# Dealing out anew the work of the opening stage of a hybrid attention layer in fp32

## The chip, the cores and the metric

One core of a Trainium2 chip runs the whole layer. The metric is the device time in microseconds (us). The engines are TensorE (PE, with its weight loads PEld), VectorE (DVE), ScalarE (ACT), GpSimd (POOL) and SyncE (SP), which here issues nearly all DMAs.

## What is computed

```
h = rms_norm(x, g_pre);  proj = h @ w_in        # 512 tokens, D = 2048
mkv = rms_norm(mem, g_mem) @ w_mem_kv           # 256 memory tokens, 4 heads of K and V
A: 6 heads, block-sparse causal attention with a T5 bias
B: 6 heads, log_f = log_sigmoid(fb + b_forget), c = cumsum(log_f),
   causal softmax(q k^T * scale + c_i - c_j) v
C: 4 heads, attention into the 256 memory tokens
y = concat(A * silu(ga), B * silu(gb), C * silu(gm));  out = x + rms_norm(y @ w_out, g_post)
```

## The kernel before, in words

**Precision and products.** Every fp32 operand is split in a high part (fp32r) and the rest. A matmul of full precision is three (lines 674 to 676: high by high, low by high, high by low). ScalarE makes the high part of a weight piece of 128 x 1024 (L1018), VectorE subtracts it for the low part (L1429), both into one of three ring slots; each slot's high part waits for the product three earlier (`used`).

**Large loop.** Projections are made by a seven-product scheme over halves of rows and columns (TOK_A to TOK_G), for 28 pairs of columns; pairs 0 to 3 are the memory heads' q and gate. A product is 8 x 3 matmuls. VectorE also adds the weight sums (L1456) and ScalarE and VectorE move partial results (c_ps is seeded from d_ps, L1116). During pair p the attention of the pair before runs between products. For memory heads: scores after product A, row maxima on VectorE after A, exp on ScalarE at B, reciprocal and normalisation at C, transposes after E, high and low parts of pT at E, probability times V (L821) after G, the gate product `gated` (L1556) on VectorE.

**Opening.** PE turns the memory tokens (8 banks, L741); ScalarE scales and writes their high part (`hi_memory`, L1075), VectorE the low part (`lo_memory`, L1516). Then eight strips (STRIPS_MEM) give K and V of the memory tokens: `strip(t)` waits for `mem_free`, which says that the PSUM bank of two strips before was read (k_mem, L1665, for strips 0 to 3; vT, L1601, `copy_v_mem`, for 4 to 7). Beside strips 3 to 6 the x tokens are turned by quarters (`turn_tiles`, `TURN_DURING`; from the twelfth bank on a turn waits for `bank_taken` of four banks before) and both engines take them from PSUM (`take_tokens`, L1089 to L1097 on ScalarE, L1533 on VectorE). Squares of a token tile (L1060) and its scaling (L1508) lie in strips 0 to 4. In strip t ScalarE makes the high part of the first piece of strip t+1, copies k_mem to kmv (L1226, after `mem_free`), then makes the second high part; VectorE does k_mem, scaling, the low part of kmv, then both low parts. The memory norms are spread over columns by one PE matmul after strip 1's first half (L853), from rstd_diag (L1695).

**Late tokens.** TOK_B, C, E, G are sums of quarters, split in high and low parts of 128 x 2048 by `hi_late` (L1106) and `lo_late` after the strips, in the order of LATE_ORDER; G - C is made at L1713. Between them stand the turned V of the memory heads (`hi_v_mem`, `lo_v_mem`).

**Forget gates.** wf holds the weights, cleared by a memset (L1700), in four parts; PE multiplies A, D, F and E tokens by them (L883) before pair 0. ScalarE copies 6 rows (L1258), VectorE forms z (L1722), POOL works out -|z| (L1939, L1940), ScalarE takes exp (L1272), POOL adds 2 (L1943), VectorE takes the reciprocal (L1744, end of pair 1), POOL runs a series of 20 operations of 6x512 (L1945 to L1953), and VectorE scans (L1747, end of pair 3).

The order on each engine is written out by hand; an engine works strictly in that order, so what stands behind a wait waits too.

Of the kernel before, what the change touches and what calls it, by code (L numbers as in the profile page):

```python
# [15 lines left out]
P = 128  # L16
# [55 lines left out]
LATE_ORDER = [TOK_E, TOK_B, TOK_C, TOK_G]  # L72
# [104 lines left out]
def build(nc, x, mem, w_in, b_forget, w_mem_kv, w_out, g_pre, g_post, g_mem, rel_bias, buckets, out):  # L177
    ctx = ExitStack()
    with ctx:
# [59 lines left out]
        wf, _ = place("wf", [P, 4, KH, 38], F32R, at=vT_at + 4 * NMEM)  # L239
# [108 lines left out]
        f_rec = sem("f_rec")  # L348
# [322 lines left out]
        def _(pe):  # L671
# [9 lines left out]
            def strip(t, between):  # L681
# [3 lines left out]
                for half in range(2):  # L685
                    pe.wait_ge(lo_done, 2 * t + half + 1)
                    w = weights(2 * t + half)
                    for k in range(KH):
                        kt = KH * half + k
                        last = three(d_ps[t % 2][:, 0:NMEM], (w[:, 0, k], w[:, 1, k]), (memT[:, 0, kt], memT[:, 1, kt]),  # L690
                                     kt == 0, kt == KT - 1)
# [184 lines left out]
            pe.wait_ge(bank_taken, TURNS)  # L876
# [139 lines left out]
        def _(act):  # L1016
# [62 lines left out]
            def take_tokens(pair, half):  # L1079

                for b in range(4 * half, 4 * half + 4):
                    act.wait_ge(bank_turned, 8 * pair + b + 1)
                    for j in range(2):
# [12 lines left out]
                        else:  # L1096
                            last = act.activation(tok[:, WHOLE[TOK_F], 0, k], src, ACTF.Copy, scale=g)  # L1097
                    last.then_inc(bank_hi, 1)

            def hi_late(i):  # L1100
                if i == LATE_ORDER[0]:
                    act.wait_ge(used, MEM_PIECES)
                    act.wait_ge(bank_taken, TURNS)
                if i == TOK_G:
                    act.wait_ge(late_f32, 1)
# [110 lines left out]
            for t in range(STRIPS_MEM):  # L1216
# [10 lines left out]
                hi_next(1)  # L1227
                if t == 0:
# [189 lines left out]
        def _(dve):  # L1418
# [91 lines left out]
            def lo_memory(half):  # L1510

                for b in range(4 * half, 4 * half + 4):
# [9 lines left out]
            def take_tokens(pair, half):  # L1522

                for b in range(4 * half, 4 * half + 4):
                    dve.wait_ge(bank_hi, 8 * pair + b + 1)
                    for j in range(2):
# [8 lines left out]
                        if (pair, half) != (2, 0):  # L1535
                            i, by = {(1, 0): (TOK_A, g_neg), (1, 1): (TOK_D, g), (2, 1): (TOK_F, g)}[(pair, half)]
# [118 lines left out]
            dve.tensor_scalar(gains_neg[:], gains[:, 1], -1.0, None, ALU.mult).then_inc(gain_negated, 1)  # L1655
            for t in range(STRIPS_MEM):
                if t == 1:
# [347 lines left out]
```

## Time and profile before

| | us |
|---|---|
| median of 3 runs | 935.55 |
| lowest, highest | 934.09, 936.16 |
| the profiled execution's own time | 932.82 |
| its span, first to last instruction | 931.0 |

The mean granted clock of TensorE was 0.987 of full speed. The profile covers one execution; its stretch from 0 to about 94 us is the opening, from there to 215.7 lie the memory pairs 0 to 4. Instructions are given as start, duration, engine, line, operation, out<-in and, in brackets, how long the engine was idle before and what ended that. An instruction's duration includes some 0.1 us in which the next has already begun on VectorE and ScalarE; costs of a list of work are taken from start to start.

### The profile page before, as it was taken

What the parts mean: (1) busy time and instruction counts of PE and PEld (TensorE: products, weight loads), DVE (VectorE), ACT (ScalarE), POOL (GpSimd) and SP (SyncE); (2) the same over time, 40 slices, a digit from 0 to 9 for tenths busy, and PEclk for the clock granted to TensorE, in tenths of its full rate; (3) what the DMA queues carried; (4) which work ended last, traced back from release to release, by engine and by line L of the source; (5) the groups of instructions that cost most, each with busy time, mean ns of one, the idle gap of its engine ahead of it and who ended that gap; (6) DMA issues with size and microseconds to landing.
All of it is one profiled execution on the core that took longest, in us unless ns stands there. A gap on an engine that the chain in (4) does not pass through costs nothing.

```text
span 931.0 us, 16276 instructions
## 1 busy us (share of the span) xinstructions
PE 887.5 (95%) x6525; PEld 839.5 (90%) x6525; DVE 728.4 (78%) x997; ACT 503.4 (54%) x882; POOL 76.7 (8%) x71
## 2 busy tenths in 40 slices
PE   7997998999999999999999999999999998889994
PEld 5887998999999999999999999999999886667873
DVE  5889878888777777777777777777777758998967
ACT  5785555555545454555555555555464645644452
POOL 0000408600000000000010202010111000000000
PEclk9998999999999999999999999999999998999998
DMA  9951424343333433343434343525252897276664
GB/s 301 294 136 46 147 58 103 102 115 102 103 102 104 102 103 102 103 103 102 110 96 114 91 122 83 134 72 144 73 146 59 281 300 239 58 269 238 227 237 168
DMA packets 166673, 130.08 MB, mean 140 GB/s; under 512 B 6393, under 2 KB 143257, under 8 KB 165446
## 3 DMA queue, kind: packets, MB, share of 16 engines
q1 hardware_dynamic: 166310, 127.99, 47.6%
q8 instruction: 52, 0.85, 0.4%
q10 hardware_dynamic: 288, 1.05, 0.4%
q14 instruction: 23, 0.19, 0.1%
HBM read 120.87 MB, written 9.73 MB: 140 GB/s over the span
## 4 chain that ended last, share of the span: by engine, by line
PE 73%; DVE 16%; ACT 5%; issue 4%; DMA 2%; DVEq 0%; POOL 0%; ACTq 0%; POOLq 0%
PE d_ps L674 11%; PE d_ps L676 11%; PE d_ps L675 11%; PE e_ps L674 6%; PE e_ps L676 6%; PE e_ps L675 6%; DVE ring L1429 5%; PE c_ps L674 3%; PE c_ps L676 3%; PE c_ps L675 3%; PE pt_ps L821 3%; DMA raw<-in_w_out_dram 2%; DVE sums L1456 1%; ACT ring L1018 1%; PE score_ps L675 1%
## 5 line engine op out<-in xcount | busy, mean ns | idle before, releaser
L1429 DVE TENSOR_TENSOR ring<-sums,ring 128x1024 fp32r<-128x1024 f32 x121 | 151.1, 1249 | 98.4 <-ACT ring L1018 97.8
L1429 DVE TENSOR_TENSOR ring<-raw,ring 128x1024 fp32r<-128x1024 f32 x131 | 161.3, 1235 | 59.5 <-ACT ring L1018 59.0
L674 PE MATMUL d_ps<-tok_hi,ring 128*128 128x256 f32 x672 | 191.8, 285 | 2.9 <-DVE ring L1429 2.9
L676 PE MATMUL d_ps<-tok_lo,ring 128*128 128x256 f32 x672 | 190.8, 284 | 0.0
L675 PE MATMUL d_ps<-tok_hi,ring 128*128 128x256 f32 x672 | 190.7, 284 | 0.0
L1018 ACT ACTIVATE ring<-raw 128x1024 fp32r<-128x1024 f32 x131 | 137.9, 1058 | 76.7 <-PE d_ps L676 36.2
L1018 ACT ACTIVATE ring<-sums 128x1024 fp32r<-128x1024 f32 x121 | 127.4, 1053 | 26.1 <-DVE sums L1456 17.7
L674 PEld LDWEIGHTS d_ps<-tok_hi,ring 128*128 128x128 f32 x672 | 129.4, 193 | 3.3 <-issue 3.3
L675 PEld LDWEIGHTS d_ps<-tok_hi,ring 128*128 128x128 f32 x672 | 129.5, 193 | 0.0
L676 PEld LDWEIGHTS d_ps<-tok_lo,ring 128*128 128x128 f32 x672 | 129.5, 193 | 0.0
L1456 DVE TENSOR_TENSOR sums<-raw 128x1024 f32<-128x1024 f32 x56 | 69.9, 1248 | 0.1
L1456 DVE TENSOR_TENSOR sums<-sums,raw 128x1024 f32<-128x1024 f32 x56 | 69.9, 1248 | 0.0
L674 PE MATMUL c_ps<-tok,ring 128*128 128x256 f32 x224 | 64.4, 288 | 0.0
L674 PE MATMUL e_ps<-tok_hi,ring 128*128 128x256 f32 x224 | 64.3, 287 | 0.0
L674 PE MATMUL e_ps<-tok,ring 128*128 128x256 f32 x224 | 64.3, 287 | 0.0
L676 PE MATMUL e_ps<-tok_lo,ring 128*128 128x256 f32 x224 | 63.4, 283 | 0.0
L675 PE MATMUL d_ps<-tok,ring 128*128 128x256 f32 x224 | 63.4, 283 | 0.0
L676 PE MATMUL d_ps<-tok,ring 128*128 128x256 f32 x224 | 63.4, 283 | 0.0
L676 PE MATMUL c_ps<-tok,ring 128*128 128x256 f32 x224 | 63.4, 283 | 0.0
L674 PE MATMUL d_ps<-tok,ring 128*128 128x256 f32 x224 | 63.4, 283 | 0.0
L675 PE MATMUL e_ps<-tok_hi,ring 128*128 128x256 f32 x224 | 63.4, 283 | 0.0
L675 PE MATMUL c_ps<-tok,ring 128*128 128x256 f32 x224 | 63.4, 283 | 0.0
(337 smaller groups left out, 2198.9 us busy)
## 6 DMA issues: line engine op xcount, KB each, us to landing
raw<-in_w_in_dram SPq DMA_DIRECT2D x112, 512.0 KB, 5.5
raw<-in_w_out_dram SPq DMA_DIRECT2D x48, 512.0 KB, 5.2
raw<-in_w_mem_kv_dram SPq DMA_DIRECT2D x16, 512.0 KB, 8.4
stage<-in_x_dram SPq DMA_DIRECT2D x4, 1024.0 KB, 9.5
xres<-in_x_dram SPq DMA_DIRECT2D x4, 1024.0 KB, 7.4
out_dram<-o_sb SPq DMA_DIRECT2D x16, 256.0 KB, 2.6
y_dram<-ybuf SPq DMA_DIRECT2D x15, 256.0 KB, 2.3
sums<-in_w_out_dram SPq DMA_DIRECT2D x6, 512.0 KB, 6.8
```

The source lines that it names most:

```text
L674: pe.matmul(dst, lhs[0], rhs[0], start=start, stop=False, skip_group_check=True)
L675: pe.matmul(dst, lhs[1], rhs[0], start=False, stop=False, skip_group_check=True)
L676: return pe.matmul(dst, lhs[0], rhs[1], start=False, stop=stop, skip_group_check=True)
L821: last = pe.matmul(bank[:, first:S], v, pT[:, hl_p, kb, first:S] if not head.memory else pT_mem[:, hl_p, kb, first:S], start=(hl_v, hl_p, ...
L1018: act.activation(dst, src, ACTF.Copy).then_inc(hi_done, 1)
L1429: return dve.tensor_tensor(dst, a_, hi_.bitcast(F32), ALU.subtract)
L1456: dve.tensor_tensor(sum_tile(p, s), one, two, ALU.add).then_inc(sum_done, 1)
```

## The change

- PE waits for the memory tokens by bank in strip 0, not for four and for eight banks; VectorE makes the first weight pieces' low parts between the banks.
- In strips 1 to 7 VectorE makes the low part of the first piece of the next strip ahead of everything else (`lo_next(t, 0)`).
- The two table copies go from VectorE to ScalarE (strip 5). wf moves to other space and POOL clears it, after 16 turned banks.
- Of the last token quarter (2, 1) ScalarE writes F's high part and C from PSUM; VectorE then does E - C and F's low part as two whole operations; C + B follows after the strips. LATE_ORDER is B, C, E, G.
- The forget gates' E part goes behind pair 0's product D; the copy and z behind product E, the exp behind product G.
- The series goes from POOL to VectorE, one operation (12 in all; scalar and tensor steps fused) after each product of pair 2 and the first five of pair 3.

```diff
-LATE_ORDER = [TOK_E, TOK_B, TOK_C, TOK_G]
+LATE_ORDER = [TOK_B, TOK_C, TOK_E, TOK_G]
...
-        wf, _ = place("wf", [P, 4, KH, 38], F32R, at=vT_at + 4 * NMEM)
+        wf, _ = place("wf", [P, 4, KH, 38], F32R, at=pT_at)
...  PE
                         kt = KH * half + k
+                        if t == 0 and k % 2 == 0:
+                            pe.wait_ge(bank_taken, kt // 2 + 1)
...
-                if t == 0:
-                    pe.wait_ge(bank_taken, 8)
...
-            pe.wait_ge(bank_taken, 4)
...
-            pe.wait_ge(bank_taken, TURNS)
+            pe.wait_ge(bank_hi, TURNS)
             pe.wait_ge(wf_ready, 1)
...
             turn_v_mem(NM - 1)
+            pe.wait_ge(bank_taken, TURNS)
             forget_gates(3, TOK_F, slice(T2, S))
             pe.wait_ge(v_ready, NM - 1)
             pe.matmul(c_ps[:, 0:T2], tok[:, 0, 0, 0, 0:P], tok[:, 0, 0, 0], start=True, stop=True)
-            pe.wait_ge(late_ready, 1)
-            forget_gates(2, TOK_E, slice(T2, S), final=True).then_inc(f_done, 1)
...
                     product(p, i)
+                    if p == 0 and i == TOK_D:
+                        pe.wait_ge(late_ready, LATE_ORDER.index(TOK_E) + 1)
+                        forget_gates(2, TOK_E, slice(T2, S), final=True).then_inc(f_done, 1)
                     attention(p, i)
...  ACT
                         else:
-                            last = act.activation(tok[:, WHOLE[TOK_F], 0, k], src, ACTF.Copy, scale=g)
+                            act.activation(tok[:, WHOLE[TOK_F], 0, k], src, ACTF.Copy, scale=g)
+                            last = act.activation(token_f32(TOK_C)[:, k], src, ACTF.Copy, scale=g)
...
                 hi_next(1)
+                if t == NM + 1:
+                    for i, (bank, lo_, hi_) in enumerate(table_banks):
+                        act.wait_ge(table_made, i + 1)
+                        act.activation(table[:, lo_:hi_], bank[0:NA, 0:hi_ - lo_], ACTF.Copy).then_inc(table_copied, 1)
...
-            hi_late(TOK_E)
             hi_v_mem(2)
+            hi_late(TOK_B)
             hi_operand(0, 2)
-            hi_late(TOK_B)
             hi_v_mem(3)
             hi_late(TOK_C)
+            hi_late(TOK_E)
             hi_late(TOK_G)
-            act.wait_ge(f_done, 1)
-            act.activation(fbuf[:, 1], f_ps[32:32 + NB, :], ACTF.Copy).then_inc(f_low, 1)
...
-                if p == 0 and i == TOK_D:
+                if p == 0 and i == TOK_E:
+                    act.wait_ge(f_done, 1)
+                    act.activation(fbuf[:, 1], f_ps[32:32 + NB, :], ACTF.Copy).then_inc(f_low, 1)
+                if p == 0 and i == TOK_G:
                     act.wait_ge(f_neg, 1)
                     act.activation(fbuf[:, 1], fbuf[:, 2], ACTF.Exp).then_inc(f_exp, 1)
...  DVE
+                if (pair, half) == (2, 1):
+                    dve.wait_ge(bank_hi, TURNS)
+                    dve.tensor_tensor(token_f32(TOK_E), token_f32(TOK_E), token_f32(TOK_C), ALU.subtract
+                                      ).then_inc(late_f32, 1)
+                    minus(tok[:, WHOLE[TOK_F], 1], token_f32(TOK_C), tok[:, WHOLE[TOK_F], 0]).then_inc(bank_taken, 4)
+                    return
...
-                        if (pair, half) == (2, 1):
-                            scaled(token_f32(TOK_C)[:, k], g, token_f32(TOK_B)[:, k], ALU.add)
-                            last = scaled(token_f32(TOK_E)[:, k], g_neg, token_f32(TOK_E)[:, k], ALU.add)
...
-            lo_memory(0)
+            lo_memory(0, 2)
             lo_mem(0)
+            lo_memory(2, 4)
             lo_mem(1)
-            lo_memory(1)
+            lo_memory(4, 8)
...
+            def lo_next(t, half):
+                if t + 1 < STRIPS_MEM:
+                    lo_mem(2 * (t + 1) + half)
+                else:
+                    add_weights(0, half + 1)
+                    lo_operand(0, half)
+
             for t in range(STRIPS_MEM):
+                if t > 0:
+                    lo_next(t, 0)
...
-                for half in range(2):
-                    if t + 1 < STRIPS_MEM:
-                        lo_mem(2 * (t + 1) + half)
-                    else:
-                        add_weights(0, half + 1)
-                        lo_operand(0, half)
-                if t == NM + 1:
-                    for i, (bank, lo_, hi_) in enumerate(table_banks):
-                        dve.wait_ge(table_made, i + 1)
-                        dve.tensor_copy(table[:, lo_:hi_], bank[0:NA, 0:hi_ - lo_]).then_inc(table_copied, 1)
+                if t == 0:
+                    lo_next(t, 0)
+                lo_next(t, 1)
...
-                    dve.memset(wf[:].bitcast(F32), 0.0).then_inc(wf_cleared, 1)
...
+            lo_v_mem(2)
             dve.wait_ge(bank_taken, TURNS)
-            dve.tensor_tensor(token_f32(TOK_G), token_f32(TOK_G), token_f32(TOK_C), ALU.subtract).then_inc(late_f32, 1)
-            lo_late(TOK_E)
-            lo_v_mem(2)
-            lo_operand(0, 2)
+            dve.tensor_tensor(token_f32(TOK_C), token_f32(TOK_C), token_f32(TOK_B), ALU.add).then_inc(late_f32, 1)
             lo_late(TOK_B)
             lo_v_mem(3)
+            lo_operand(0, 2)
+            dve.wait_ge(late_f32, 2)
+            dve.tensor_tensor(token_f32(TOK_G), token_f32(TOK_G), token_f32(TOK_C), ALU.subtract).then_inc(late_f32, 1)
             lo_late(TOK_C)
+            lo_late(TOK_E)
             lo_late(TOK_G)
-            dve.wait_ge(f_low, 1)
-            dve.scalar_tensor_tensor(out=fbuf[:, 0], in0=f_ps[0:NB, :], scalar=bfor[:, 0:1], in1=fbuf[:, 1],
-                                     op0=ALU.add, op1=ALU.add).then_inc(f_z, 1)
+            def forget_series(n):
...
+                elif n < last - 1:
+                    dve.scalar_tensor_tensor(out=p, in0=p, scalar=SERIES[n - 2], in1=s2, op0=ALU.add, op1=ALU.mult
+                                             ).then_inc(f_series, 1)
...
+                if p == 0 and i == TOK_E:
+                    dve.wait_ge(f_low, 1)
+                    dve.scalar_tensor_tensor(out=fbuf[:, 0], in0=f_ps[0:NB, :], scalar=bfor[:, 0:1], in1=fbuf[:, 1],
+                                             op0=ALU.add, op1=ALU.add).then_inc(f_z, 1)
...
+                if 2 <= p < NM:
+                    forget_series(PRODUCTS * (p - 2) + i)
...  POOL
+            pool.wait_ge(bank_turned, 16)
+            pool.memset(wf[:].bitcast(F32), 0.0).then_inc(wf_cleared, 1)
...
-            pool.wait_ge(f_rec, 1)
-            chain(pool.tensor_tensor(e, e, p, ALU.mult))
-            chain(pool.tensor_tensor(s2, e, e, ALU.mult))
-            chain(pool.tensor_scalar(p, s2, SERIES[0], None, ALU.mult))
-            for c in SERIES[1:]:
-                chain(pool.tensor_scalar(p, p, c, None, ALU.add))
-                chain(pool.tensor_tensor(p, p, s2, ALU.mult))
...
```

## Rows read from the trace of the kernel before

**Rows 1.** The page's part 1: engine, busy us, share of the span, instructions

```profile
PE 887.5 (95%) x6525; PEld 839.5 (90%) x6525; DVE 728.4 (78%) x997; ACT 503.4 (54%) x882; POOL 76.7 (8%) x71
```

**Rows 2.** Timeline of PE in the opening: start, duration, instruction, [idle before, releaser]

```profile
20.48 0.39 PE L674 MATMUL d_ps<-memT,ring 128*128 128x256 f32 x1 [1.50 <-DVE memT L1516]
...
26.88 0.70 PE L853 MATMUL c_ps<-rstd_diag,ones 128*128 128x256 f32 x2 [0.39 <-DVE rstd_diag L1695]
...
80.26 0.69 PE L751 MATMUL c_ps<-ident,vT 128*128 128x128 f32 x2 [2.39 <-DVE vT L1601]
...
90.20 0.58 PE L892 MATMUL c_ps<-tok 128*128 128x256 f32 x1 [2.30 <-DVE kmv L1429]
```

**Rows 3.** Timeline of DVE in strip 1

```profile
27.62 0.42 DVE L1660 COPY rstd_mem<-c_ps 128x256 f32<-128x256 f32 x1 [0.79 <-PE c_ps L853]
...
30.84 2.35 DVE L1429 TENSOR_TENSOR ring<-raw,ring 128x1024 fp32r<-128x1024 f32 x2
```

**Rows 4.** Timeline of ACT, strips 1 to 6

```profile
27.44 1.04 ACT L1018 ACTIVATE ring<-raw 128x1024 fp32r<-128x1024 f32 x1
...
51.13 0.40 ACT L1226 ACTIVATE kmv<-k_mem 128x256 fp32r<-128x256 f32 x1
...
52.39 0.45 ACT L1092 ACTIVATE tok<-score_ps,gains 128x256 fp32r<-128x256 f32 x1
...
58.09 2.11 ACT L1018 ACTIVATE ring<-raw 128x1024 fp32r<-128x1024 f32 x2
...
67.39 1.06 ACT L1018 ACTIVATE ring<-raw 128x1024 fp32r<-128x1024 f32 x1 [2.81 <-PE d_ps L676]
```

**Rows 5.** Timeline of DVE, end of the opening and start of the large loop

```profile
79.81 0.40 DVE L1601 TENSOR_TENSOR vT<-d_ps,rstd_mem 128x256 f32<-128x256 f32 x1
...
85.34 2.27 DVE L1713 TENSOR_TENSOR tok_f<-tok_f 128x2048 f32<-128x2048 f32 x1
...
98.15 0.73 DVE L1722 SCALAR_TENSOR_TENSOR fbuf<-pt_ps,bfor,fbuf 6x512 f32<-6x512 f32 x1
...
99.94 1.21 DVE L1429 TENSOR_TENSOR ring<-raw,ring 128x1024 fp32r<-128x1024 f32 x1
```

**Rows 6.** Timeline of PE: first matmuls of pair 0's products D and E

```profile
102.42 0.28 PE L674 MATMUL c_ps<-tok,ring 128*128 128x256 f32 x1
...
105.30 0.28 PE L674 MATMUL d_ps<-tok_hi,ring 128*128 128x256 f32 x1
```

**Rows 7.** Stretch 91 to 94: length, busy (count) by engine, granted clock, DMA, GB/s

```profile
91.00:94.00 3.00, 3.00 (x17) 2.62 (x16) 3.00 (x4) 0.41 (x2) 0.00 (x0) 0.58 0.02 5
```

**Rows 8.** Timeline of POOL: the forget gates' first two operations

```profile
98.97 6.24 POOL L1939 TENSOR_SCALAR fbuf<-fbuf 6x512 f32<-6x512 f32 x1 [96.47 <-DVE fbuf L1722]
105.29 1.28 POOL L1940 TENSOR_TENSOR fbuf<-fbuf 6x512 f32<-6x512 f32 x1
```

**Rows 9.** Timeline of PE: first matmul of product A, pairs 1 to 4

```profile
113.94 0.28 PE L674 MATMUL d_ps<-tok,ring 128*128 128x256 f32 x1
...
137.79 0.28 PE L674 MATMUL d_ps<-tok,ring 128*128 128x256 f32 x1
...
166.69 0.28 PE L674 MATMUL d_ps<-tok,ring 128*128 128x256 f32 x1
...
191.81 0.28 PE L674 MATMUL d_ps<-tok,ring 128*128 128x256 f32 x1
```

**Rows 10.** DVE groups by shape, 142.7 to 178: count, busy, mean ns, idle before

```profile
L1429 DVE TENSOR_TENSOR ring<-sums,ring 128x1024 fp32r<-128x1024 f32 x4 | 7.5, 1890 | 0.0
```

**Rows 11.** Timeline of DVE: first sums of pairs 2 and 4, pT of pair 4

```profile
144.63 1.73 DVE L1456 TENSOR_TENSOR sums<-raw 128x1024 f32<-128x1024 f32 x1
...
196.90 1.22 DVE L1456 TENSOR_TENSOR sums<-raw 128x1024 f32<-128x1024 f32 x1
...
212.65 1.28 DVE L1429 TENSOR_TENSOR pT_mem<-pt_ps,pT_mem 128x512 fp32r<-128x512 f32 x2
```

**Rows 12.** Timeline of PE: probability times V in pair 4

```profile
214.27 1.55 PE L821 MATMUL pt_ps<-pT_mem,kmv 128*128 128x512 f32 x6
```

More of the change, by code:

```diff
@@ L347, in build @@
         f_den = sem("f_den")
-        f_rec = sem("f_rec")
+        f_series = sem("f_series")
         f_pool = sem("f_pool")
@@ L1508, in scale_tile, with lo_memory @@
                 dve.tensor_scalar(one, one, stat[:, 4, t:t + 1], None, ALU.mult).then_inc(tile_scaled, 1)
-            def lo_memory(half):
-                for b in range(4 * half, 4 * half + 4):
+            def lo_memory(b0, b1):
+                for b in range(b0, b1):
                     dve.wait_ge(bank_hi, b + 1)
@@ L1533, in scaled @@
                             return dve.scalar_tensor_tensor(out=dst, in0=src, scalar=by, in1=other, op0=ALU.mult, op1=op)
-                        if (pair, half) != (2, 0):
-                            i, by = {(1, 0): (TOK_A, g_neg), (1, 1): (TOK_D, g), (2, 1): (TOK_F, g)}[(pair, half)]
+                        if pair == 1:
+                            i, by = {(1, 0): (TOK_A, g_neg), (1, 1): (TOK_D, g)}[(pair, half)]
                             last = scaled(tok[:, WHOLE[i], 1, k], by, tok[:, WHOLE[i], 0, k].bitcast(F32), ALU.subtract)
@@ L1711, in _ @@
             copy_v_mem(STRIPS_MEM - 1)
+            lo_v_mem(2)
             dve.wait_ge(bank_taken, TURNS)
-            dve.tensor_tensor(token_f32(TOK_G), token_f32(TOK_G), token_f32(TOK_C), ALU.subtract).then_inc(late_f32, 1)
-            lo_late(TOK_E)
-            lo_v_mem(2)
-            lo_operand(0, 2)
+            dve.tensor_tensor(token_f32(TOK_C), token_f32(TOK_C), token_f32(TOK_B), ALU.add).then_inc(late_f32, 1)
             lo_late(TOK_B)
             lo_v_mem(3)
+            lo_operand(0, 2)
+            dve.wait_ge(late_f32, 2)
+            dve.tensor_tensor(token_f32(TOK_G), token_f32(TOK_G), token_f32(TOK_C), ALU.subtract).then_inc(late_f32, 1)
             lo_late(TOK_C)
+            lo_late(TOK_E)
             lo_late(TOK_G)
-            dve.wait_ge(f_low, 1)
-            dve.scalar_tensor_tensor(out=fbuf[:, 0], in0=f_ps[0:NB, :], scalar=bfor[:, 0:1], in1=fbuf[:, 1],
-                                     op0=ALU.add, op1=ALU.add).then_inc(f_z, 1)
+            def forget_series(n):
+                z, e, s2, p = fbuf[:, 0], fbuf[:, 1], fbuf[:, 2], fbuf[:, 3]
+                last = len(SERIES) + 3
+                if n > last:
+                    return
+                dve.wait_ge(f_series, n + 1)
+                if n == 0:
+                    dve.tensor_tensor(e, e, p, ALU.mult).then_inc(f_series, 1)
+                elif n == 1:
+                    dve.tensor_tensor(s2, e, e, ALU.mult).then_inc(f_series, 1)
+                elif n == 2:
+                    dve.tensor_scalar(p, s2, SERIES[0], None, ALU.mult).then_inc(f_series, 1)
+                elif n < last - 1:
+                    dve.scalar_tensor_tensor(out=p, in0=p, scalar=SERIES[n - 2], in1=s2, op0=ALU.add, op1=ALU.mult
+                                             ).then_inc(f_series, 1)
+                elif n == last - 1:
+                    dve.scalar_tensor_tensor(out=p, in0=p, scalar=1.0, in1=e, op0=ALU.add, op1=ALU.mult
+                                             ).then_inc(f_series, 1)
+                else:
+                    dve.wait_ge(f_pool, 4)
+                    dve.tensor_tensor(z, p, z, ALU.subtract).then_inc(f_parts, 1)
             def before_operand(p, i):
@@ L1741, in after_operand @@
                     second_strip(p, i)
+                if p == 0 and i == TOK_E:
+                    dve.wait_ge(f_low, 1)
+                    dve.scalar_tensor_tensor(out=fbuf[:, 0], in0=f_ps[0:NB, :], scalar=bfor[:, 0:1], in1=fbuf[:, 1],
+                                             op0=ALU.add, op1=ALU.add).then_inc(f_z, 1)
                 if p == 1 and i == TOK_G:
                     dve.wait_ge(f_den, 1)
-                    dve.reciprocal(fbuf[:, 3], fbuf[:, 3]).then_inc(f_rec, 1)
+                    dve.reciprocal(fbuf[:, 3], fbuf[:, 3]).then_inc(f_series, 1)
+                if 2 <= p < NM:
+                    forget_series(PRODUCTS * (p - 2) + i)
                 if p == NM - 1 and i == TOK_G:
@@ L1943, in _ @@
             pool.tensor_scalar(p, e, 2.0, None, ALU.add).then_inc(f_den, 1)
-            pool.wait_ge(f_rec, 1)
-            chain(pool.tensor_tensor(e, e, p, ALU.mult))
-            chain(pool.tensor_tensor(s2, e, e, ALU.mult))
-            chain(pool.tensor_scalar(p, s2, SERIES[0], None, ALU.mult))
-            for c in SERIES[1:]:
-                chain(pool.tensor_scalar(p, p, c, None, ALU.add))
-                chain(pool.tensor_tensor(p, p, s2, ALU.mult))
-            chain(pool.tensor_scalar(p, p, 1.0, None, ALU.add))
-            chain(pool.tensor_tensor(p, p, e, ALU.mult))
-            pool.tensor_tensor(z, p, z, ALU.subtract).then_inc(f_parts, 1)
             for a in range(NA, NAB):
```

6 lines of the change are left out of this document (3 added, 3 removed).

## The prediction

> **What bounds the kernel now.** I read the page's busy shares first: TensorE (PE) is busy for 887.5 of 931.0 us [rows 1], so a change outside the large loop can only touch PE's pauses. Then PE's timeline, for those pauses. One product of 24 matmuls takes 2.88 us (105.30 - 102.42) [rows 6], and most starts are exactly that far apart. The opening holds four pauses of note: 1.50 us before the second half of strip 0, 0.39 before the spread of the norms, 2.39 before the third turn of V, 2.30 before the marker matmul of L892 [rows 2]. After the last two PE ran at the lower clock level: 17 matmuls in 3.0 us at a granted clock of 0.58, a loss of 3.0 x 0.42 = 1.26 us each [rows 7]. The memory pairs start at 113.94, 137.79, 166.69 and 191.81 [rows 9]: 23.85 us for pair 1, 28.90 for pair 2, 25.12 for pair 3. In pairs 2 and 3 GpSimd (POOL) runs the forget gates' series (lines 1946 to 1953), and VectorE's (DVE) ring parts take 1890 ns [rows 10] where two took 2.27 us from start to start elsewhere (31-33 us) [rows 3]. So I put 5.05 + 1.27 = 6.32 us down to the series.
>
> My sum is made against the profiled execution, 932.82 us with a span of 931.0, which lies 2.7 under the median of 935.55; the difference carries over.
>
> **Waits by bank.** VectorE makes the first ring part after two banks, and PE starts strip 0 by bank. Half 0 ends some 2 us sooner, half 1 too (before, PE waited 1.50 for all banks) [rows 2]. But strip 1's second half stands behind the spread at 26.88, which waited for rstd_diag [rows 2], and VectorE's list up to it is the same from its second ring part on. The pause moves there: 0.
>
> **VectorE's ring part ahead of k_mem (strips 1 to 4).** The part needs ScalarE's (ACT) high part, which ScalarE writes after the squares; k_mem now queues behind it, and ScalarE's kmv copy waits for k_mem. Before, ScalarE went from high part to kmv to the next high part (51.13 straight behind it) [rows 4]. Now it idles for a VectorE ring part and k_mem, 1.14 + 0.46 = 1.6 us, in each of four strips. In strips 1 to 3 part of that lies where it waited for PE before. Walked through with the durations of [rows 3, 4]: in strip 1 the high part ends at 28.40, kmv moves to 30.48; strip 2's kmv to 36.56; strip 3's to 42.61; strip 4's from 51.13 to 54.45. The token quarter (1,1) starts at 55.7, not 52.39 [rows 4]: 3.3 late. Its last bank frees at 62.35, PE's turn (2,0) ends at 62.9 (before 59.7).
>
> **Table copies to ScalarE, clearing of wf to POOL.** Copies: 0.8 us on ScalarE (estimate from the 6x512 step's 0.73) [rows 5]. They come off VectorE's list (0.9), which idles soon after: 0. The memset runs from about 51, beside VectorE's idle wait for strip 4's high part; bounds 0 and 0.7 (one ring part's excess, 1890 - 1200 ns) [rows 10]; I take 0. The Trainium skill, "SBUF — State Buffer", Who interferes with whom, says that a two-input VectorE operation contends only with a GpSimd one that reads SBUF, not with one that only writes; by that it is 0 as well, and no row here shows a memset beside VectorE.
>
> **Last token quarter.** ScalarE now makes 16 copies, 5.70 us as in (1,1) (58.09 - 52.39) [rows 4], not 8. Its high part before it waits for PE's strip 6 (67.39 before [rows 4], now 69.1); tokens run from 70.3 to 76.0. VectorE's whole-tile E-C waits for all of them: it idles from 71.6 to 76.1, then E-C and F low, 2.2 each by the 2048-wide sum [rows 5], end at 80.5; before, 24 narrow operations ended at 79.81 [rows 5]. Loss 0.7.
>
> **Late tokens.** From 79.81 to the start of the main loop's D part at 99.94 VectorE had no pause [rows 5]; that includes f_z, 0.7. It now does C+B more (2.2) and f_z less: D's part starts at 80.5 + 20.1 + 2.2 - 0.7 = 102.2 and PE's D at 103.5 (1.36 us after its start, as at 30.84 to 32.20). Before: 102.42 [rows 6]. **+1.05.**
>
> **Forget gates' E part** moves behind D. PE starts its A earlier (91.0, the 2.30 pause and 16 matmuls gone) but stops before D from 99.8 to 103.5. So the place freed ahead of A is given back. The 16 matmuls at the pace of [rows 6] are 1.92: **+1.92**; and after so long a pause I count the lower clock once, as after 2.30 [rows 2, 7]: **+1.2** (bounds 0 and 2.5). PE's E starts at 109.6, not 105.30.
>
> **The chain to exp.** Let T be the end of that E. VectorE writes f_z at T+3.3 (last_two, a sum, a ring part). POOL's L1939 took 6.24 and L1940 1.28 [rows 8]: f_neg at T+10.9. ScalarE comes to its wait for f_neg at T+6.8, behind the high part of product G; queued behind it are exp (1.9 with its table load), both tanh, the seed of c_ps and D's high part; VectorE waits for the tanh. The seed lands at T+13.8, PE wants it at T+12.96; the row maxima, exps and probabilities of pair 1 follow late, and PE's probability-times-V, wanted at T+28.2, starts at T+30.3: **+2.1**. Bounds: 0, if L1939's 6.24 is 2.5 here (it was the first of its kind), and 3.
>
> **Series to VectorE.** Twelve operations of 6x512, six or seven of them in each of pairs 2 and 3. The profile has none of these from SBUF alone; nearest is L1722, 0.73 long, 0.66 to the next [rows 5]; bounds 0.33 (half its length) and 1.2. I take 0.6. The clean pair is tight: its pT parts end at 213.9, PE's L821 starts at 214.27 [rows 11, 12], slack 0.35, and 0.5 more lies before the ring part that waits for ScalarE. Pair 2: five series steps lie ahead of its pT (2.7), the reciprocal makes its first sum 1.75 later than a clean pair's (144.63 - 137.79 against 196.90 - 191.81) [rows 9, 11], the late exp 0.55 more; less 0.34 (no kv part), 0.35 and 0.5: 3.9 lost, before 5.05: **-1.15**. Pair 3: steps 7 to 11 and what is left of 5 and 6, 3.2 less 1.2: 2.05 lost, before 1.27: **+0.8**.
>
> **Sum**: 1.05 + 1.92 + 1.2 + 2.1 - 1.15 + 0.8 = +5.9 us: 938.7 for a profiled execution, **941.4** by the median.
>
> **Rivals.**
> *A, faster: VectorE has the room.* If ScalarE's strips 1 to 4 are not late (the 1.6 us gaps fall where it waited anyway) and whole-tile sums keep VectorE ahead, PE's D doesn't stop. Then A's earlier start counts: -2.8 (93.8 to 91.0), +1.92 for the E part behind D, and POOL's contention goes, -6.3, with about 2 given back in pairs 2 and 3. That is -5.2: 930.4 by the median. It decides once VectorE's D part is ready by 99.8, 2.4 before what I find. For it: [rows 10], and the 2.30 pause [rows 2]; against: VectorE without a pause from 79.81 to 99.94 [rows 5]. The Trainium skill, "Perfetto Trace Analysis", Optimizing Scalar/DVE Operations, says that with VectorE saturated, moving work to ScalarE may make sense; by that rule this rival holds, and no row yet shows it.
>
> *B, no change.* ScalarE is late, but the exp costs nothing (POOL's first operation short, terms 2.1 and 0.55 gone) and D's pause keeps the clock (1.2 gone), with series steps nearer 0.5: 5.9 - 4.6 = +1.3, 936.9.
>
> *C, slower still.* PE's turn (2,0) now waits bank by bank, 57.4 to 62.9, and strip 5 then starts at the low level: 1.2 on the whole chain to D, through the high part that waits for PE [rows 4]: +7.1, 942.7. It lies in my range.
>
> **How the numbers follow.** About 0.2% (1.9 us) is what a measurement of this kernel can tell from no change. Forecast with C: 0.60 (own range 938 to 945, by the bounds of exp, series and clock). B, and mixtures within 1.9 us of no change: 0.20. A and milder gains: 0.20. The range runs to 932.5, to take in the milder part of A and all of B, and to 945. That the ring order loses ScalarE time follows from the order of waits; what is least sure is how much of it reaches D.
>
> **What would show it.** ScalarE's kmv copies idle about 1.6 us each for k_mem; the token quarter (1,1) starts near 55.7; VectorE idles 4 us before E-C; PE pauses over 3 us before pair 0's D, and E starts near 109.6; ScalarE waits over 3 us for f_neg; no inflated ring parts in pairs 2 and 3, yet pairs of about 27.7 and 25.9 us. I am wrong if D starts without a pause, or if pairs 2 and 3 are near 24 us.

## The result and the profile after

The changed kernel takes 940.45 us (median of 5 runs, 939.31 to 940.62) where the kernel before takes 935.55 (934.09 to 936.53): a ratio of 1.0051, 95% interval 1.0037 to 1.0066. It is slower by 4.9 us. The forecast was 941.4 in a range of 932.5 to 945.0. The profiled execution took 940.52 us, span 938.4. That of the kernel before lay 2.7 us under its median, which is why the spans differ by 7.4 and the medians by 4.9: up to pair 4 the two traces differ by 5.31 us (197.12 against 191.81), the rest arose behind the opening and the memory pairs, in code the change does not touch. 0.6 of the 5.31 is there from the first banks on, before the change begins to act: ScalarE starts on the memory tokens at 10.30, not 9.67. In the fourteen profiled executions of this document that start lies anywhere from 9.40 to 10.75, so it belongs to the execution rather than to the change (9.76 in a variant of the changed kernel).

PE's timeline of the changed kernel (start, duration, instruction, [idle before, releaser]). The first, second and fourth line answer to [rows 2], the fifth and sixth to [rows 6], the last four to [rows 9]; the third is strip 5's second half:

```profile
18.87 0.36 PE L674 MATMUL d_ps<-memT,ring 128*128 128x256 f32 x1 [1.61 <-DVE memT L1523]
...
27.52 0.70 PE L855 MATMUL c_ps<-rstd_diag,ones 128*128 128x256 f32 x2 [2.05 <-DVE rstd_diag L1708]
...
64.16 0.56 PE L674 MATMUL d_ps<-memT,ring 128*128 128x256 f32 x1
...
86.30 0.69 PE L753 MATMUL c_ps<-ident,vT 128*128 128x128 f32 x2 [3.86 <-DVE vT L1611]
...
106.50 0.39 PE L674 MATMUL c_ps<-tok,ring 128*128 128x256 f32 x1 [2.91 <-DVE ring L1436]
...
111.36 0.28 PE L674 MATMUL d_ps<-tok_hi,ring 128*128 128x256 f32 x1
...
120.00 0.28 PE L674 MATMUL d_ps<-tok,ring 128*128 128x256 f32 x1
...
143.85 0.28 PE L674 MATMUL d_ps<-tok,ring 128*128 128x256 f32 x1
...
171.24 0.28 PE L674 MATMUL d_ps<-tok,ring 128*128 128x256 f32 x1
...
197.12 0.28 PE L674 MATMUL d_ps<-tok,ring 128*128 128x256 f32 x1
```

Read it from the top. The pause before the spread of the norms has grown from 0.39 to 2.05: what strip 0 gained went there. Strip 5's second half starts at 64.16 (59.68 before). Pair 0's D starts at 106.50 behind a pause of 2.91, its E at 111.36, 6.06 later than before. From there on pair 1 takes 23.85 us as before, pair 2 27.39 (28.90 before), pair 3 25.88 (25.12 before).

ScalarE's timeline shows where the lateness is made; it answers to [rows 4]:

```profile
31.22 0.42 ACT L1228 ACTIVATE kmv<-k_mem 128x256 fp32r<-128x256 f32 x1 [2.09 <-DVE k_mem L1685]
...
37.38 0.42 ACT L1228 ACTIVATE kmv<-k_mem 128x256 fp32r<-128x256 f32 x1 [1.63 <-DVE k_mem L1685]
...
55.54 0.42 ACT L1228 ACTIVATE kmv<-k_mem 128x256 fp32r<-128x256 f32 x1 [1.63 <-DVE k_mem L1685]
...
56.82 0.45 ACT L1093 ACTIVATE tok<-score_ps,gains 128x256 fp32r<-128x256 f32 x1
...
71.94 1.06 ACT L1019 ACTIVATE ring<-raw 128x1024 fp32r<-128x1024 f32 x1 [2.03 <-PE d_ps L676]
...
121.33 1.28 ACT L1279 ACT_TABLE_LOAD   x1
123.76 0.63 ACT L1279 ACTIVATE fbuf<-fbuf 6x512 f32<-6x512 f32 x1 [1.14 <-POOL fbuf L1982]
```

The last two rows are the gates' exp and the loading of its table, which belong to the chain to exp below. In each of strips 1 to 4 ScalarE stands idle for k_mem, and quarter (1,1) starts at 56.82, 4.4 later than before. VectorE's timeline, against [rows 5]:

```profile
79.14 2.29 DVE L1533 TENSOR_TENSOR tok_f<-tok_f 128x2048 f32<-128x2048 f32 x1 [4.56 <-ACT tok_f L1099]
81.35 2.29 DVE L1436 TENSOR_TENSOR tok<-tok_f,tok 128x2048 fp32r<-128x2048 f32 x1
83.56 1.22 DVE L1463 TENSOR_TENSOR sums<-raw 128x1024 f32<-128x1024 f32 x1
...
105.24 1.22 DVE L1436 TENSOR_TENSOR ring<-raw,ring 128x1024 fp32r<-128x1024 f32 x1
...
153.12 0.67 DVE L1744 TENSOR_TENSOR fbuf<-fbuf 6x512 f32<-6x512 f32 x1
```

E-C waits 4.56 us for ScalarE's sixteen copies. From 79.14 to D's ring part at 105.24 VectorE has no pause: that list sets D. A series step is 0.67 long, 0.60 to the next (153.12 to 153.72).

Two stretches of the same kernel (length, busy with count for PE, PEld, DVE, ACT, POOL, then granted clock, DMA share, GB/s), against [rows 7]:

```profile
64.00:68.00 4.00, 4.00 (x24) 4.00 (x23) 4.00 (x8) 4.00 (x12) 0.00 (x0) 0.57 0.46 110
...
106.50:109.50 3.00, 3.00 (x25) 3.00 (x26) 3.00 (x3) 1.24 (x2) 0.00 (x0) 1.00 1.03 269
```

After the spread-out turns (pauses of 1.31, 0.81 and 0.80 between 60 and 64) strip 5 runs at a granted clock of 0.57, mostly the lower level: its second half takes 6.07 us (64.16 to 70.23), where the same work at full clock takes 4.61 (below). After the pause before D the clock is full. And POOL, against [rows 8]:

```profile
52.43 1.11 POOL L1978 MEMSET wf<- 128x1216 f32 x1 [49.92 <-PE pt_ps L743]
117.87 3.97 POOL L1981 TENSOR_SCALAR fbuf<-fbuf 6x512 f32<-6x512 f32 x1 [64.32 <-DVE fbuf L1778]
121.92 1.81 POOL L1982 TENSOR_TENSOR fbuf<-fbuf 6x512 f32<-6x512 f32 x1
```

Not all of this belongs to the kernel. The kernel with the series back on POOL (below) has the same code as the changed one up to the end of pair 1, so its trace is a second execution of the same opening:

```profile
64.54:68.54 4.00, 4.00 (x36) 4.00 (x35) 4.00 (x8) 4.00 (x13) 0.00 (x0) 1.00 0.50 116
...
105.41:109.41 4.00, 4.00 (x21) 4.00 (x22) 3.77 (x4) 1.23 (x2) 0.00 (x0) 0.60 1.02 263
```

Here strip 5 kept the full clock (64.54 to 69.15, 4.61 us), D started at 105.41 behind a pause of 3.52, and D ran mostly at the lower level: E followed 6.33 us after D's start, not 4.86. Both executions lose 1.5 us once, in different places, and counted from ScalarE's first bank both reach E after some 101.0 us (101.06 here, 100.99 there). So a difference of 1.5 us at one point of two traces can be the clock of that execution. Where it matters below, the granted clock is given beside the comparison.

### The profile page after: what moved, and what is told of

Same layout as the page of the kernel before. It is cut to its first block, busy times and chain, and to the rows that moved or that the text cites. A ratio compares the mean times of both kernels' runs of the same rounds, so it can differ in the third digit from the quotient of the medians.

```text
span 938.4 us, 16256 instructions
## 1 busy us (share of the span) xinstructions
PE 891.0 (95%) x6525; PEld 841.7 (90%) x6525; DVE 723.6 (77%) x985; ACT 507.5 (54%) x892; POOL 43.5 (5%) x52
## 3 DMA queue, kind: packets, MB, share of 16 engines
q10 hardware_dynamic: 288, 1.05, 0.3%
## 4 chain that ended last, share of the span: by engine, by line
PE 72%; DVE 15%; ACT 6%; issue 5%; DMA 1%; POOL 1%; DVEq 0%; ACTq 0%; POOLq 0%
PE d_ps L674 11%; PE d_ps L676 11%; PE d_ps L675 11%; PE e_ps L674 5%; PE e_ps L676 5%; PE e_ps L675 5%; DVE ring L1436 5%; PE c_ps L674 3%; PE c_ps L676 3%; PE c_ps L675 3%; PE pt_ps L823 3%; DVE sums L1463 2%; ACT ring L1019 2%; PE score_ps L675 1%; PE score_ps L674 1%
## 5 line engine op out<-in xcount | busy, mean ns | idle before, releaser
L1436 DVE TENSOR_TENSOR ring<-sums,ring 128x1024 fp32r<-128x1024 f32 x121 | 148.6, 1228 | 96.6 <-ACT ring L1019 95.9
L674 PE MATMUL c_ps<-tok,ring 128*128 128x256 f32 x224 | 64.4, 287 | 2.9 <-DVE ring L1436 2.9
L674 PE MATMUL e_ps<-tok,ring 128*128 128x256 f32 x224 | 64.3, 287 | 0.0
L676 PE MATMUL c_ps<-tok,ring 128*128 128x256 f32 x224 | 63.4, 283 | 0.0
L676 PE MATMUL e_ps<-tok,ring 128*128 128x256 f32 x224 | 63.4, 283 | 0.0
```

Source lines behind the costliest of these rows:

```text
L674: pe.matmul(dst, lhs[0], rhs[0], start=start, stop=False, skip_group_check=True)
L676: return pe.matmul(dst, lhs[0], rhs[1], start=False, stop=stop, skip_group_check=True)
L1436: return dve.tensor_tensor(dst, a_, hi_.bitcast(F32), ALU.subtract)
```

## The experiments

All twelve were timed in five rounds beside the kernel before. Ratios are to that kernel (935.40, 934.94 and 935.51 us in the three groups), with 95% intervals.

### Waits by bank alone (on the kernel before)

```diff
+                        if t == 0 and k % 2 == 0:
+                            pe.wait_ge(bank_taken, kt // 2 + 1)
-            lo_memory(0); lo_mem(0); lo_mem(1); lo_memory(1)
+            lo_memory(0, 2); lo_mem(0); lo_memory(2, 4); lo_mem(1); lo_memory(4, 8)
```

> The kernel before with PE's waits by bank in strip 0 and VectorE's first ring parts between the banks, and nothing else. Theory: strip 0 ends some 2.4 us sooner, PE then waits that much longer for the spread of the norms (pause of 0.4 before, about 2.4 now), nothing behind it moves: 935.4, within 1 us. Rival (an earlier strip 0 frees the ring and brings the whole opening forward): 933.0 to 933.5.

Measured 935.22, ratio 1.0003 (0.9993 to 1.0014): no difference. PE's row at the spread:

```profile
27.77 0.70 PE L855 MATMUL c_ps<-rstd_diag,ones 128*128 128x256 f32 x2 [2.05 <-DVE rstd_diag L1695]
```

The gain of strip 0 is a longer pause one strip on. By the medians this part is worth nothing.

### The ring part ahead of k_mem: alone, and taken out

Alone, on the kernel before:

```diff
             for t in range(STRIPS_MEM):
+                if t > 0:
+                    lo_next(t, 0)
...
+                if t == 0:
+                    lo_next(t, 0)
+                lo_next(t, 1)
```

> The kernel before with VectorE's ring part ahead of k_mem and the scaling in strips 1 to 7, and nothing else of the change. Theory (ScalarE and VectorE wait for each other in turn): ScalarE idles 1.6 us before each kmv copy, token quarter (1,1) starts near 55.7 instead of 52.39, and as VectorE's list behind it has no pause, pair 0 starts 3 us or more later: about 939. Rival (the part ahead helps PE in strips 2 and 3 and the lateness is absorbed): 934 to 935.5.

Measured 936.70, ratio 1.0022 (1.0011 to 1.0033): slower by 1.8 us, less than the expected 4. ScalarE's rows:

```profile
30.84 0.42 ACT L1226 ACTIVATE kmv<-k_mem 128x256 fp32r<-128x256 f32 x1 [2.08 <-DVE k_mem L1674]
...
37.01 0.42 ACT L1226 ACTIVATE kmv<-k_mem 128x256 fp32r<-128x256 f32 x1 [1.63 <-DVE k_mem L1674]
...
43.16 0.42 ACT L1226 ACTIVATE kmv<-k_mem 128x256 fp32r<-128x256 f32 x1 [1.62 <-DVE k_mem L1674]
...
55.17 0.42 ACT L1226 ACTIVATE kmv<-k_mem 128x256 fp32r<-128x256 f32 x1 [1.63 <-DVE k_mem L1674]
```

The idle times are those of the changed kernel to 0.01. The quarter starts at 56.44, pair 0 at 96.36 (93.79 before), 2.6 later where 3 or more were expected; 0.3 of it is the execution's later start. Pair 4 starts 2.9 later in the traces, while the medians say 1.8.

Taken out of the changed kernel (k_mem first, both ring parts behind it):

> The changed kernel with VectorE's ring part behind k_mem and the scaling again (strips 1 to 7), all else as changed. Theory (the ring part ahead of k_mem makes ScalarE idle 1.6 us in each of strips 1 to 4): no idle before the kmv copies, token quarter (1,1) starts about 3.3 us sooner than in the changed kernel (56.82 there), PE's turn (2,0) is not spread out and strip 5 doesn't run at the low clock level (1.5 us), so pair 0's E starts about 4.7 us sooner and the median is about 935.8. Rival (ScalarE had room there; the loss comes from the larger last quarter and the moved gates' part alone): the quarter starts sooner, yet E does not by more than 1 us: 939.5 to 940.5.

Measured 936.62, ratio 1.0012 (0.9999 to 1.0025), 3.8 us less than the changed kernel: by the medians most of the loss, though less than the 4.7 expected. PE's row before D and the stretch from it on:

```profile
102.40 0.58 PE L674 MATMUL c_ps<-tok,ring 128*128 128x256 f32 x1 [3.52 <-DVE ring L1436]
```

```profile
102.40:107.60 5.20, 5.20 (x24) 5.20 (x25) 3.77 (x4) 1.23 (x2) 0.00 (x0) 0.50 0.88 238
```

D starts 4.1 us sooner than in the changed kernel, but in this execution all its 24 matmuls run at the lower level (clock 0.50): 5.3 us instead of 3.0. E starts at 109.66, only 1.7 us sooner, not 4.7, and pair 4 too is 1.7 sooner. The expected full clock in strip 5 is there (1.00 from 61.8 to 65.8), but strip 2 lost as much in this execution (0.60 from 33 to 37, 1.00 in the kernel before). The trace thus accounts for 1.7 of the 3.8; the rest of the difference between the two profiled executions lies behind the memory pairs, in code that is the same.

### The last quarter dealt as before

```diff
-                            last = act.activation(token_f32(TOK_C)[:, k], src, ACTF.Copy, scale=g)
+                            (VectorE: F low, C+B and E-C per k, 24 operations of 256)
-            (C += B after the strips)
```

> The changed kernel with the last token quarter dealt as before (ScalarE writes F's high part alone, VectorE 24 narrow operations that make C+B and E-C too), all else as changed. Theory (whole operations behind all banks cost VectorE its wait of 4.6 us, and C+B comes on top): VectorE's list to pair 0's D ends 1.8 to 2.5 us sooner than in the changed kernel, about 938.4. Rival (ScalarE's larger share did relieve VectorE): 942 or more.

Measured 938.76, ratio 1.0033 (1.0021 to 1.0046): 1.7 us less than the changed kernel, with intervals that overlap (the changed kernel's begins at 1.0037). It is not more, as it would be if ScalarE's larger share had relieved VectorE. D starts at 104.36 there (106.50 in the changed kernel), but most of these 2.1 us are strip 5, which kept the full clock in this execution. Against the kernel with the series back on POOL, which kept it too, D is 1.05 sooner, 0.86 without the different start: VectorE's list became shorter by that much, not by the 1.8 to 2.5 expected.

### The gates' E part back ahead of pair 0

```diff
+LATE_ORDER = [TOK_E, TOK_B, TOK_C, TOK_G]
+            pe.wait_ge(late_ready, 1)                      # ahead of pair 0
+            forget_gates(2, TOK_E, slice(T2, S), final=True).then_inc(f_done, 1)
-                    if p == 0 and i == TOK_D: forget_gates(...)
+            (copy, z at the end of the late tokens, exp at product D)
```

> The changed kernel with the gates' E part, the order of the late tokens, the copy, z and the exp where they were before the change, all else as changed. Theory (the move behind D gives back ahead of E what it frees ahead of A, since D waits for VectorE's list either way): E starts within 1 us of the changed kernel's 111.4, the median is 939.5 to 941. Rival (the move itself is what costs the 5 us): about 936.

Measured 938.51, ratio 1.0029 (1.0018 to 1.0041): 1.9 us less than the changed kernel, more than I gave the move, with intervals that just overlap (1.0037 to 1.0066 there). E starts at 110.76 (111.36 changed), within the expected microsecond; 0.54 of these 0.6 us are the earlier start of the execution (9.76 against 10.30), so ahead of E the move gives back what it frees. Pair 2's first pause is 0.56 there and 0.88 in the changed kernel. The trace accounts for some 0.4 of the 1.9 beyond the start; the rest is not explained. The move is not what costs most of the 5 us, and it does not pay either.

### Clearing and table copies alone (on the kernel before)

wf lies in its new place here too.

```diff
-                    dve.memset(wf[:].bitcast(F32), 0.0).then_inc(wf_cleared, 1)
+            pool.memset(wf[:].bitcast(F32), 0.0).then_inc(wf_cleared, 1)
-                        dve.tensor_copy(table[:, lo_:hi_], ...)
+                        act.activation(table[:, lo_:hi_], ..., ACTF.Copy)
```

> The kernel before with the clearing of wf on GpSimd and the table copies on ScalarE, and nothing else. Theory (VectorE's list from 59 us to pair 0's D has no pause, so 1.9 us taken off it come off the time, where VectorE doesn't wait for ScalarE as in the changed kernel): about 933.4. Rival (VectorE then waits for ScalarE's token copies instead, as I counted for the changed kernel): 935.0 to 935.5.

Measured 933.54, ratio 0.9979 (0.9965 to 0.9993): 2.0 us faster. The trace shows it only when the clock is looked at, for D starts at 102.46, as before (102.42). In this execution strip 2 ran at a lower granted clock than in that of the kernel before (this kernel first):

```profile
33.00:37.00 4.00, 4.00 (x24) 4.00 (x24) 3.86 (x10) 0.81 (x2) 0.00 (x0) 0.61 1.14 311
```

```profile
33.00:37.00 4.00, 4.00 (x36) 4.00 (x35) 3.86 (x10) 2.07 (x4) 0.00 (x0) 1.00 1.15 317
```

With 0.3 of later start this brings token quarter (1,1) to 54.21, 1.8 later than before. From there to D it takes 48.25 us against 50.03, so 1.8 us of VectorE's list came off. Work taken off that list pays where it has no pause. In the changed kernel VectorE waits for ScalarE behind it (4.56 us), which should swallow the 2 us; that was not tested by taking this part out of the changed kernel.

### The series: back on POOL, by product, in the pause

Back on POOL, in the changed kernel:

> The changed kernel with the forget gates' series back on POOL (20 operations), all else as changed. Theory (contention of POOL with VectorE costs pairs 2 and 3 some 6.3 us, as before the change, and the series on VectorE costs them 5.6): ring parts of 1.5 to 1.9 us in pairs 2 and 3, the median within 1 us of the changed kernel, about 941.2. Rival (the slow pairs before were not POOL's doing): ring parts of 1.2 us, pairs 2 and 3 of 24 us each, about 935.

Measured 941.10, ratio 1.0052 (1.0034 to 1.0070), the changed kernel's time within 0.7 us. VectorE's ring parts from pair 2's start to pair 4's, in the changed kernel and in this one:

```profile
L1436 DVE TENSOR_TENSOR ring<-sums,ring 128x1024 fp32r<-128x1024 f32 x9 | 10.9, 1211 | 0.0
```

```profile
L1436 DVE TENSOR_TENSOR ring<-sums,ring 128x1024 fp32r<-128x1024 f32 x9 | 13.6, 1518 | 0.0
```

With POOL at the series a ring part takes 1.52 us in the mean, not 1.21, and pairs 2 and 3 take 29.16 and 25.12 us, not 27.39 and 25.88. Two different costs of nearly the same size stand against each other.

On VectorE with a step after each product, on the kernel before:

```diff
+                if 2 <= p < NM:
+                    forget_series(PRODUCTS * (p - 2) + i)
```

> The kernel before with the series on VectorE as in the change, one step after each product of pairs 2 and 3, and nothing else. Theory (each step stands in VectorE's list ahead of something PE waits for): pairs 2 and 3 take about 27.4 and 25.9 us (28.9 and 25.1 before), the median is about 934.8, hardly faster than before. Rival (VectorE has room, only contention was lost): 23.9 us each, 929.2.

Measured 933.92, ratio 0.9984 (0.9973 to 0.9995), 1.5 us faster. On VectorE, where it waits for ScalarE anyway:

```diff
                     if i == 2:
                         invert(head, 0)
                         invert(head, 1)
+                        if p == 1:   (wait f_den, reciprocal)
+                        if 2 <= p < NM:
+                            for n in range(5 * (p - 2), 5 * (p - 1)):
+                                forget_series(n)
...  (steps 10 and 11 ahead of the scan)
```

> The kernel before with the series on VectorE, but its steps put where VectorE waits 2.9 us for ScalarE anyway, behind the reciprocals of the row sums at product C: the gates' reciprocal in pair 1, five steps each in pairs 2 and 3, the last two ahead of the scan. Theory: the pause takes them at nothing, pairs 1 to 3 take 23.9 to 24.3 us each and pair 4 up to 24.4; the median is about 929.7. Rival (the steps cost wherever they stand, by VectorE's total work): about 934.8 as with a step per product.

Measured 929.82, ratio 0.9941 (0.9922 to 0.9961): 5.6 us faster than before, by one of the change's parts, put elsewhere. The same steps after each product gave 1.5. One more thing moved with them: the gates' reciprocal of 3.33 us, which stood on VectorE at the end of pair 1 (139.52 in the kernel with a step per product) and now fills pair 1's pause (126.98). VectorE's timeline in pair 2 of this kernel:

```profile
150.69 0.22 DVE L1638 RECIPROCAL rinv<-rowsum 128x2 f32<-128x2 f32 x2
150.82 0.66 DVE L1733 TENSOR_TENSOR fbuf<-fbuf 6x512 f32<-6x512 f32 x1
151.52 0.68 DVE L1735 TENSOR_TENSOR fbuf<-fbuf 6x512 f32<-6x512 f32 x1
152.23 0.41 DVE L1737 TENSOR_SCALAR fbuf<-fbuf 6x512 f32<-6x512 f32 x1
152.68 1.39 DVE L1739 SCALAR_TENSOR_TENSOR fbuf<-fbuf 6x512 f32<-6x512 f32 x2
154.00 1.21 DVE L1429 TENSOR_TENSOR ring<-raw,ring 128x1024 fp32r<-128x1024 f32 x1
```

In a clean pair 3.1 us lie between the start of the row sums' reciprocals and the next ring part (205.09 to 208.24 in pair 4 of the kernel before), 2.93 of them idle; five steps fill them. PE's starts of pairs 2, 3 and 4, first of this kernel, then of the one with a step per product:

```profile
137.41 0.28 PE L674 MATMUL d_ps<-tok,ring 128*128 128x256 f32 x1
...
161.27 0.28 PE L674 MATMUL d_ps<-tok,ring 128*128 128x256 f32 x1
...
185.11 0.28 PE L674 MATMUL d_ps<-tok,ring 128*128 128x256 f32 x1
```

```profile
137.93 0.28 PE L674 MATMUL d_ps<-tok,ring 128*128 128x256 f32 x1
...
165.00 0.28 PE L674 MATMUL d_ps<-tok,ring 128*128 128x256 f32 x1
...
190.87 0.28 PE L674 MATMUL d_ps<-tok,ring 128*128 128x256 f32 x1
```

Pairs of 23.86 and 23.84 us against 27.07 and 25.87. Pair 4 then takes 24.7 in the first (185.11 to 209.79) instead of 23.85, with the two steps ahead of the scan. Pair 3's 2.0 us are the place of the steps alone; in pair 2's 3.2 the moved reciprocal has a share that no run separates.

### Three versions that mend the change

The changed kernel with k_mem first, the series in the pause, and VectorE's work on the last quarter by bank:

```diff
-                    dve.wait_ge(bank_hi, TURNS)
-                    (E-C and F low, 2 operations of 2048)
+                    for b in range(4, 8):
+                        dve.wait_ge(bank_hi, 16 + b + 1)
+                        (E-C and F low of this bank's two k, 2 operations of 512)
```

> The changed kernel with k_mem first again, the last quarter's E-C and F low part made by bank (8 operations of 512 wide, each as soon as ScalarE has its bank) instead of two behind all banks, and the series in the pause at product C. Theory (VectorE idles 4.5 us before E-C and everything to pair 0's D hangs on its list): VectorE is through with the quarter 3.2 us sooner than with k_mem first alone, D and E come 3.2 us sooner or more (what the low clock cost), pairs 2 and 3 lose at most 0.5 instead of 5.6: about 928. Rival (the narrow operations cost what the idle gives): 931.5.

Measured 929.66, ratio 0.9946 (0.9929 to 0.9963), 1.7 over the expectation. VectorE's waits for the banks are 0.17 us each and the quarter ends at 76.3 as meant, yet D starts at 99.25 behind a pause of 3.52 and in the profiled execution again runs at the lower level, 5.28 us for its 24 matmuls. That execution took 932.40, 2.7 above the median, with a mean clock of 0.982; the four fastest (928.20 to 928.83) had 0.987 to 0.989, so the loss need not be in each. Next, G's parts behind D's and the gates in that pause:

```diff
-                    if p == 0 and i == TOK_D:
+                    if p == 0 and i == TOK_C:
                         (gates' E part)
-            hi_late(TOK_G) / lo_late(TOK_G)      # ahead of pair 0
+            (behind pair 0's products C and D)
```

> As the kernel with the quarter by bank, and besides G's high and low parts behind pair 0's products C and D instead of ahead of pair 0, and the gates' E part between products C and D, where PE waits for VectorE, instead of between D and E. Theory: VectorE's part for D is ready 2.2 us sooner, the 16 gate matmuls (1.9 us) lie in PE's pause, D starts near 97, E near 100 (105.3 before the change), the median is about 924. Rival (PE's pause before D is not VectorE's list but something else, the seed of c_ps or the ring): less than 1 us better than by bank alone, about 927.5.

Measured 926.99, ratio 0.9906 (0.9887 to 0.9924), 3 over the expectation. The pause before D is gone (D at 97.96, at full clock); one of 2.33 before product C stays, and pair 1 takes 25.4 us, as ScalarE waits for -|z| from POOL, 1.93 beyond the loading of the exp's table. Last, the gates' copy and z at product D:

```diff
-                if p == 0 and i == TOK_E:
+                if p == 0 and i == TOK_D:
                     (copy on ScalarE, z on VectorE)
```

> As the kernel with the gates ahead of D, and ScalarE's copy of the gates and z behind product D instead of E. Theory (in that kernel ScalarE waits 1.9 us for -|z| from GpSimd, pair 1 takes 25.4 us instead of 23.9): -|z| comes about 3 us sooner, that wait goes, pair 1 takes 23.9 to 24.2 us, about 925.7. Rival (G's low part, now behind z, becomes late for product G): no gain, 927 or more.

Measured 925.46, ratio 0.9890 (0.9871 to 0.9910): 10 us faster than the kernel before and 15 faster than the changed one. PE in this kernel, from product C of pair 0 to the start of pair 2:

```profile
93.15 0.36 PE L674 MATMUL d_ps<-tok_hi,ring 128*128 128x256 f32 x1 [2.32 <-issue]
...
107.60 0.39 PE L674 MATMUL d_ps<-tok_hi,ring 128*128 128x256 f32 x1 [0.82 <-DVE last_two L1583]
110.57 0.28 PE L674 MATMUL d_ps<-tok,ring 128*128 128x256 f32 x1
...
134.42 0.28 PE L674 MATMUL d_ps<-tok,ring 128*128 128x256 f32 x1
```

Pair 1 is back at 23.85. The expected rival shows a little as well: product G now waits 0.82.

## Why the prediction was right, and where it was not

The sum was +5.9, the medians differ by 4.9 and the traces at pair 4 by 5.3. Its parts, one by one:

- **Waits by bank: 0.** Right, and shown alone (1.0003).
- **Ring part ahead of k_mem.** The mechanism is as predicted, to the number: 1.6 us of idle per strip was the forecast, 1.63, 1.62 and 1.63 were measured (2.09 in strip 1). By the medians taking it out is worth 3.8 us of the 4.9; put in alone it costs 1.8, and the traces differ by 1.7 and 2.9 at pair 4. That it is the largest single cost is shown, its size only within these bounds.
- **Clearing and copies: 0** was the forecast for the changed kernel, where VectorE waits for ScalarE; no run took this part alone out of it. That they bring 2.0 us without that wait I had not looked for.
- **Last quarter and late tokens: +1.05 at D.** This term came out at +4.08, of which 0.6 was there from the start. VectorE's list took what was forecast (79.14 to 105.24, 26.1 us; forecast 76.1 to 102.2, 26.1), but it began 3.0 later. The step that failed is the time at which ScalarE gets strip 6's piece: 69.1 forecast, 71.94 measured. 1.5 of it is strip 5 at the lower clock level, which I had set apart as rival C instead of in the sum; nearly all the rest is the late start and half a microsecond on ScalarE before quarter (1,1). Rival C thus came true in place in this execution, and its price of 1.2 was 1.5. In two other traces with the same code up to there (series on POOL, quarter as before) strip 5 kept the full clock.
- **Gates' E part behind D: +1.92.** Right: E follows 4.86 us after D's start, 1.98 more than the 2.88 before.
- **Lower clock after D's pause: +1.2.** 0 in this execution: the clock was full behind 2.91 us of idle. In the second execution of the same opening it was 1.5, and there strip 5 lost nothing. That this term and rival C come one for the other was in neither the sum nor the rivals.
- **The chain to exp: +2.1.** Wrong: pair 1 takes 23.85. The forecast was that ScalarE comes to its wait 6.8 us after E's end and -|z| 10.9 after it, 4.1 later, with exp and its table load (1.9) behind. Measured from E's end at 114.23: 7.1 and 9.5. L1981 took 3.97, not L1939's 6.24, and the table load of 1.28 ran while ScalarE waited, not behind the wait, so only 1.14 of idle is left in the row. The two are worth 1.4 and 1.3 us. The seed of c_ps landed by 125.2, PE wanted it at 127.19; forecast were 128.0 and 127.2. The lower bound of 0 is what happened, but only half for the reason given with it. That the chain can reach PE is shown by the kernel with the gates ahead of D, where pair 1 took 25.4, 1.5 more.
- **Series on VectorE: -1.15 and +0.8.** Right: pair 2 gave back 1.51, pair 3 cost 0.76 more; a step took the 0.6 assumed. The working of pair 2 counts 2.7 for five such steps, which are 3.0. The placements show that the price is not only the work but where it stands: 5.6 us gained in the pause (with the gates' reciprocal there too), 1.5 with a step per product.
- **The memset: 0.** It lay at 52.43 to 53.54, while VectorE waited for ScalarE until 53.95. What the Trainium skill, "SBUF — State Buffer", Who interferes with whom, says of it was not put to the test: no VectorE operation lay beside it.

So the total is near by luck: two terms that didn't come (3.3 together) stand against a chain to D that was 3.0 later than forecast. The sign and the main cause were right; the distribution over terms was half right.

Rival A, faster by 5.2, fell with its condition: VectorE's D part came at 105.24, not by 99.8. Its idea was sound in part: dealt out anew (k_mem first, the quarter by bank, the gates ahead of D) and with the series in the pause, the change's parts give 10 us, and the series in the pause alone gives 5.6 of them.

## What to carry to other kernels

Moving work to the less busy engine pays only if no engine then waits for it in a block: sixteen small copies followed by one whole-tile operation made VectorE idle 4.6 us, by bank it was 0.7 in all. An operation pulled ahead of one that another engine waits for can make both wait in turn at every step; look for who is queued behind each wait on both sides. And before spreading small work over a loop, look for the place in its list where the engine waits anyway: the same twelve steps were worth 1.5 us in one place and, together with a reciprocal of 3.33 us, 5.6 in the other. And before a difference between two traces is put down to an edit, compare the granted clock stretch by stretch: here two executions of the same code lost 1.5 us in different places.

## What the runs showed of the hardware

The cost of a PE pause in clock was not fixed by the pause. Behind 2.91 us before D it was nothing in the changed kernel (clock 1.00, 24 matmuls in 3.0 us). Behind 3.52 in two kernels (k_mem first, quarter by bank) the following 24 matmuls all ran at the lower level (clock 0.50, 5.3 us, so 2.3 lost); behind 3.52 in the kernel with the series on POOL they took 4.5 us, and behind 2.54 in the kernel with the old quarter 4.3. Nor was it fixed by the code: strip 5 ran at 0.57 in one execution and at 1.00 in another of the same opening, and strip 2 at 1.00 or 0.61 (kernel before, clearing and copies alone) behind a pause of 1.75 or 1.76. Such a loss can eat half of what a shorter list brings.

POOL's first two-operation step of 6x512 took 6.24 or 6.25 us in each of the seven kernels that form z ahead of pair 0 and 3.90 or 3.97 in each of the seven that form it behind product D or E, with the same work and whether or not POOL had cleared wf before. Why is open. ScalarE's loading of the exp's table (1.28 us) ran while it waited for the exp's input (121.33 in the changed kernel).
